# Attention units of half the tokens with both heads, and a residue-ordered copy of the second group's q and k, in a fused encoder block

## What is computed

```python
def dilated_band_attention(q, k, v, dilation, half, slopes):
...
    scores = jnp.einsum('bdhnqe,bdhnke->bdhnqk', qb, kb)
    scores = scores - slopes[None, None, :, None, None, None] * dist
    scores = jnp.where(valid, scores, NEG_INF)
    m = jnp.max(scores, axis=-1, keepdims=True)
    p = jnp.exp(scores - m)
    den = jnp.sum(p, axis=-1, keepdims=True)
    out = jnp.einsum('bdhnqk,bdhnke->bdhnqe', p, vb) / den
    lse = (m + jnp.log(den))[..., 0]
```

## Time and profile before

| | |
|---|---|
| median of 3 runs | 3403.81 us (3403.66 to 3404.89) |
| profiled execution | 3403.46 us, its span 3401.7 us |
| TensorE matmul busy | 3296.8 us, 97% |
| TensorE weight load busy | 2727.4 us, 80% |
| VectorE busy | 1846.6 us, 54% |
| ScalarE busy | 1301.9 us, 38% |
| GpSimd busy | 1578.1 us, 46% |
| DMA, share of 16 engines | 40.8% |

### The profile page before, as it was taken

How to read it: one execution, slowest core, us unless ns; L and a number is a source line. 1 busy time by engine, 2 the same in 40 slices (tenths; PEclk the granted TensorE clock), 3 DMA queues, 4 the chain that set the end, 5 groups by cost and what they waited for, 6 DMA issues and landing times.

```text
span 3401.7 us, 42068 instructions
## 1 busy us (share of the span) xinstructions
PE 3296.8 (97%) x15943; PEld 2727.4 (80%) x15943; DVE 1846.6 (54%) x2336; ACT 1301.9 (38%) x2131; POOL 1578.1 (46%) x1492
## 2 busy tenths in 40 slices
PE   7999999999889999999899999999999999999998
PEld 6788878788578888888578878888888888888886
DVE  3665655555666777664432023456456456455556
ACT  4534344444155665663342232233233233223222
POOL 4554533333258888886365433333333323323323
PEclk9999999999899999999899999999999999999999
DMA  5444453433355555554543323332332333323323
GB/s 170 129 142 141 142 154 116 120 112 90 91 143 136 148 135 140 125 128 122 201 143 113 123 75 100 118 106 87 112 99 88 117 93 104 107 87 111 111 81 106
DMA packets 666051, 405.06 MB, mean 119 GB/s; under 512 B 193534, under 2 KB 597178, under 8 KB 665338
## 3 DMA queue, kind: packets, MB, share of 16 engines
q1 hardware_dynamic: 665850, 402.38, 40.8%
HBM read 347.05 MB, written 54.53 MB: 118 GB/s over the span
## 4 chain that ended last, share of the span: by engine, by line
PE 49%; DVE 1%; ACT 0%; issue 0%; POOL 0%; DVEq 0%; ACTq 0%; POOLq 0%
PE f_bank L2194 9%; PE f_bank L2195 9%; PE f_bank L2196 9%; PE f_bank L2232 4%; PE f_bank L2233 4%; PE f_bank L2234 4%; PE f_bank L2172 2%; PE f_bank L2174 2%; PE f_bank L2173 2%; PE f_bank L2115 1%; PE f_bank L2116 1%; PE f_bank L2117 1%; PE f_bank L2124 0%; PE f_bank L2150 0%; DVE orw_plain L2688 0%
## 5 line engine op out<-in xcount | busy, mean ns | idle before, releaser
L2483 POOL TENSOR_TENSOR w_lo_b<-w_raw_b,w_hi_b 128x1024 fp32r<-128x1024 f32 x176 | 435.7, 2479 | 903.9 <-ACT w_hi_b L2359 903.7
L2194 PE MATMUL f_bank<-act_rounded,w_lo_b 128*128 128x512 f32 x1408 | 549.3, 390 | 1.2 <-DVE act_rounded L2595 1.2
L2195 PE MATMUL f_bank<-act_rounded,w_hi_b 128*128 128x512 f32 x1408 | 548.0, 389 | 0.0
L2196 PE MATMUL f_bank<-act_rounded,w_hi_b 128*128 128x512 f32 x1408 | 547.9, 389 | 0.0
L1294 POOL TENSOR_TENSOR ring_w_rounded<-ring_w_plain,ring_w_hi 128x1024 fp32r<-128x1024 f32 x134 | 327.3, 2447 | 463.1 <-ACT ring_w_hi L1310 463.0
L1622 PE MATMUL slab_ps<-h_hi,ring_w_rounded 128*128 128x512 f32 x1056 | 426.2, 404 | 2.7 <-DVE h_lo L1451 2.4
L1623 PE MATMUL slab_ps<-h_lo,ring_w_hi 128*128 128x512 f32 x1056 | 414.6, 393 | 0.0
L1624 PE MATMUL slab_ps<-h_hi,ring_w_hi 128*128 128x512 f32 x1056 | 414.1, 392 | 0.0
L2359 ACT CAST w_hi_b<-w_raw_b 128x1024 fp32r<-128x1024 f32 x176 | 185.0, 1052 | 452.9 <-DMA w_raw_b<-in_w_ffn_up_dram 207.1
L2194 PEld LDWEIGHTS f_bank<-act_rounded,w_lo_b 128*128 128x128 f32 x1408 | 264.7, 188 | 56.0 <-DVE act_rounded L2595 1.1
L2196 PEld LDWEIGHTS f_bank<-act_rounded,w_hi_b 128*128 128x128 f32 x1408 | 264.5, 188 | 55.1
(11 more groups left out here) (432 smaller groups left out, 6234.7 us busy)
## 6 DMA issues: line engine op xcount, KB each, us to landing
ring_w_plain<-in_w_in_dram SPq DMA_DIRECT2D x190, 512.0 KB, 4.1
w_raw_b<-in_w_ffn_gate_dram SPq DMA_DIRECT2D x88, 512.0 KB, 3.7
w_raw_b<-in_w_ffn_up_dram SPq DMA_DIRECT2D x88, 512.0 KB, 3.7
w_raw_b<-in_w_ffn_down_dram SPq DMA_DIRECT2D x42, 512.0 KB, 4.1
w_raw_b<-in_w_out_dram SPq DMA_DIRECT2D x16, 1024.0 KB, 5.1
zt<-slab_out SPq DMA_DIRECT2D x63, 256.0 KB, 4.3
hid_plain<-in_w_ffn_down_dram SPq DMA_DIRECT2D x21, 512.0 KB, 4.5
oa_plain<-in_w_ffn_down_dram SPq DMA_DIRECT2D x21, 512.0 KB, 4.3
```

Source lines behind the costliest of these rows:

```text
L2194: pe.matmul(o, wl[:, k, :], act_hi[:, kk, :], start=kk == 0, stop=False)
L2195: pe.matmul(o, wh[:, k, :], act_lo[:, kk, :], start=False, stop=False)
L2196: return pe.matmul(o, wh[:, k, :], act_hi[:, kk, :], start=False, stop=stop)
L2483: pool.tensor_tensor(low(r), slab_raw(j % 2), high(r).bitcast(F32), ALU.subtract).then_inc(slab_low, 1)
```

## The change

1. A unit is now half of the tokens (`half`, blocks `2 * half` and `2 * half + 1`) of both heads of a pair. The number of units and of matmuls per unit stays. In `scores` and `sum` the head `e` runs in the innermost loop, so neighbouring matmuls use rows (or output columns) 0 to 63 and 64 to 127 in turn. The scores of head `e`, block `i` go to `sc_ps[:, 2 * e + i]`.
2. `soft` does one addition per head (and for the first group per block), `exp` stays at four exponentials, and `file` copies 128 partitions x 256 tokens.
3. A new ScalarE stage `by_four`, once per pair behind `by_residue`, copies the second group's q and k by residue modulo 4 to `q_4` and `k_4`. It waits for `qk_landed[1]` and, from pair 1 on, for the last scores of the second group of the pair before. The scores of the second group read the copies and wait for `by_four` in place of the loads.
4. `sel_r` lies in the same place as `sel`; its copy at the start remains.

```diff
     if n is not None and n % ATT_PER_PAIR == 0:
-        stages.append(("by_residue", n // ATT_PER_PAIR))
+        stages += [("by_residue", n // ATT_PER_PAIR), ("by_four", n // ATT_PER_PAIR)]
...
+        q_4, k_4 = sb("q_4", [P, SEQ]), sb("k_4", [P, SEQ])
...
+                        if name == "by_four":
+                            act.wait_ge(qk_landed[1], 32 * (n + 1))
+                            if n:
+                                act.wait_ge(made, PE_DONE["scores", ATT_PER_PAIR * n - 3])
+                            for src, dst in ((q_sb, q_4), (k_sb, k_4)):
+                                ins = act.copy(dst[:, :].rearrange("p (r m) -> p r m", r=4),
+                                               src[1][:, :].rearrange("p (m r) -> p r m", r=4))
+                            ins.then_inc(taken_act, 1)
...
-                            for t in range(4):
-                                ins = act.activation(p_sb[n % 2][:, t, 0:nk], s_sb[:, t, 0:nk], ACT.Exp, bias=negmax[n % 2][:, t:t + 1],
-                                                     accum_out=dn_all[gr][:, 2 * j + e, t:t + 1])
+                            for e in range(2):
+                                for i in range(2):
+                                    x, t = 2 * e + i, 2 * half + i
+                                    ins = act.activation(p_sb[n % 2][:, x, 0:nk], s_sb[:, x, 0:nk], ACT.Exp, bias=negmax[n % 2][:, x:x + 1],
+                                                         accum_out=dn_all[gr][:, 2 * j + e, t:t + 1])
...
-                            parts = ([(0, 1, 0), (1, 3, 1), (3, 4, 2)] if gr == 0 else [(0, 4, 2 + gr)])
+                            for e in range(2):
+                                parts = [(0, 1, half), (1, 2, 1 + half)] if gr == 0 else [(0, 2, 2 + gr)]
...
-                            o = u_all[gr][r, j, :]
+                            o, src = u_all[gr][:, j, :], pv_ps[:, half * 2 * P:(half + 1) * 2 * P]
                             if gr == 0:
-                                dve.tensor_copy(o, pv_ps[r, :]).then_inc(taken_dve, 1)
+                                dve.tensor_copy(o[:, half * 2 * P:(half + 1) * 2 * P], src).then_inc(taken_dve, 1)
                             else:
-                                res = 4 if gr == 1 else 16
+                                res = 2 if gr == 1 else 8
...
-                            for t in range(4):
-                                if gr == 0:
-                                    w = windows(t)
-                                    ins = pe.matmul(sc_ps[:, t, :], q_sb[0][r, t * P:(t + 1) * P], k_sb[0][r, w:w + 2 * P], start=True, stop=True)
-                                else:
-                                    ins = pe.matmul(sc_ps[:, t, 0:P], tokens((q_sb[1], q_r)[gr - 1][r, :], gr, t),
-                                                    tokens((k_sb[1], k_r)[gr - 1][r, :], gr, t), start=True, stop=True)
+                            q_t, k_t = ((q_sb[0], k_sb[0]), (q_4, k_4), (q_r, k_r))[gr]
+                            for i in range(2):
+                                t = 2 * half + i
+                                at, nk = (windows(t), 2 * P) if gr == 0 else (t * P, P)
+                                for e in range(2):
+                                    r = slice(64 * e, 64 * e + 64)
+                                    ins = pe.matmul(sc_ps[:, 2 * e + i, 0:nk], q_t[r, t * P:(t + 1) * P], k_t[r, at:at + nk], start=True, stop=True)
...
-                            for t in range(4):
+                            for i in range(2):
+                                t = 2 * half + i
                                 for b in range(nb):
                                     vi = vstarts(0).index(windows(t) + b * P) if gr == 0 else t
-                                    ins = pe.matmul(pv_ps[64 * e:64 * e + 64, t * P:(t + 1) * P], v_tok[gr][:, vi, 64 * e:64 * e + 64],
-                                                    p_t[:, t * nb + b, :], start=b == 0, stop=b == nb - 1, skip_group_check=True)
+                                    for e in range(2):
+                                        ins = pe.matmul(pv_ps[64 * e:64 * e + 64, t * P:(t + 1) * P], v_tok[gr][:, vi, 64 * e:64 * e + 64],
+                                                        p_t[:, (2 * e + i) * nb + b, :], start=b == 0, stop=b == nb - 1, skip_group_check=True)
...
-            g.sel = c0.enter_context(nc.sbuf_tensor("sel", [ATTN_HPG, ATTN_HPG, HEAD_DIM], F32))
+            g.sel_r, g.sel = two_faced(nc, c0, "sel", [ATTN_HPG, ATTN_HPG, HEAD_DIM])
```

More of the change, by code:

```diff
@@ L1055, in phase_project @@
         floor, y, t_sb, kk_out = (sb(n, [P, SEQ]) for n in ("n_floor", "n_y", "n_t", "kk_out"))
-        sq_hi, ones_r, sel_r = sb("n_sq_hi", [P, SEQ], F32R), sb("ones_r", [P, P], F32R), sb("sel_r", [ATTN_HPG, ATTN_HPG * HEAD_DIM], F32R)
+        sq_hi, ones_r = sb("n_sq_hi", [P, SEQ], F32R), sb("ones_r", [P, P], F32R)
         with ExitStack() as early:
@@ L1337, in _ @@
                 act.wait_ge(att_consts, 2)
-                act.copy(sel_r[:, :], g.sel[:, :, :].rearrange("h a b -> h (a b)")).then_inc(sums_ready, 1)
+                act.copy(g.sel_r[:, :, :], g.sel[:, :, :]).then_inc(sums_ready, 1)
                 for s in range(N_SLOT):
                     for name, n in pro_act(s):
-                        if name == "by_residue":
+                        if name == "by_four":
[6 more added lines that the diff above has]
+                            ins.then_inc(taken_act, 1)
+                        elif name == "by_residue":
                             act.wait_ge(qk_landed[2], 48 * (n + 1))
@@ L1544, in _ @@
                         elif name == "soft":
-                            j, gr, e = att_unit(n)
-                            nk, h = 2 * P if gr == 0 else P, 2 * j + e
+                            j, gr, half = att_unit(n)
+                            nk = 2 * P if gr == 0 else P
                             dve.wait_ge(made, PE_DONE["scores", n])
@@ L1549, in _ @@
                                 dve.wait_ge(taken_act, ACT_DONE["exp", n - 1])
-                            parts = ([(0, 1, 0), (1, 3, 1), (3, 4, 2)] if gr == 0 else [(0, 4, 2 + gr)])
[L1551 to L1555, removed]
+                            for e in range(2):
+                                parts = [(0, 1, half), (1, 2, 1 + half)] if gr == 0 else [(0, 2, 2 + gr)]
+                                for a0, a1, dj in parts:
+                                    a0, a1 = 2 * e + a0, 2 * e + a1
+                                    ins = dve.scalar_tensor_tensor(out=s_sb[:, a0:a1, 0:nk],
+                                                                   in0=g.dist[:, dj:dj + 1, 0:nk].broadcast_to([P, a1 - a0, nk]),
+                                                                   scalar=g.slope[:, gr, 2 * j + e:2 * j + e + 1], in1=sc_ps[:, a0:a1, 0:nk],
+                                                                   op0=ALU.mult, op1=ALU.add)
@@ L1556, in _ @@
                             link(ins)
-                            link(dve.tensor_reduce(mx_all[gr][:, h, :], s_sb[:, :, 0:nk], AX.X, ALU.max))
-                            dve.tensor_scalar(negmax[n % 2][:, :], mx_all[gr][:, h, :], -1.0, None, ALU.mult).then_inc(taken_dve, 1)
+                            top = mx_all[gr][:, 2 * j:2 * j + 2, 2 * half:2 * half + 2]
+                            link(dve.tensor_reduce(top, s_sb[:, :, 0:nk].rearrange("p (e i) k -> p e i k", e=2), AX.X, ALU.max))
+                            dve.tensor_scalar(negmax[n % 2][:, :].rearrange("p (e i) -> p e i", e=2), top, -1.0, None, ALU.mult).then_inc(taken_dve, 1)
@@ L1689, in _ @@
                         elif name == "scores":
[L1690 to L1693, removed]
+                            j, gr, half = att_unit(n)
+                            if gr == 0:
+                                pe.wait_ge(qk_landed[0], 32 * (j + 1))
                             else:
-                                pe.wait_ge(taken_act, ACT_DONE["by_residue", j])
+                                pe.wait_ge(taken_act, ACT_DONE["by_four" if gr == 1 else "by_residue", j])
                             if n >= 1:
@@ L1746, in _ @@
                             pe.wait_ge(taken_dve, DVE_DONE["weigh", n - 4] if n >= 4 else DVE_DONE["share", 0])
-                            heads = sel_r[:, 2 * j * HEAD_DIM:(2 * j + 2) * HEAD_DIM]
+                            heads = g.sel_r[:, 2 * j:2 * j + 2, :].rearrange("h a b -> h (a b)")
                             pe.matmul(four_banks[n % 4], heads, m_lo[gr], start=True, stop=False)
```

12 lines of the change are left out of this document (5 added, 7 removed).

## The result

The changed kernel takes 3366.45 us (median of 4 runs, 3361.01 to 3370.11) against 3404.22 for the kernel before (3403.66 to 3404.89): ratio 0.9889, interval 0.9877 to 0.9901. That is 38 us less, where 22 were forecast (3382) with a range of 3372 to 3397. It is the rival "full overlap", for which the text worked out 3368 and gave a chance of 0.08.

A forecast was written before the change was run, and what follows sets the result against it. The prediction took TensorE to bound the kernel from 477 to 836 us and summed 3403.5 - 8.6 (copies) - 14.1 (both heads in a unit) + 1.0 (given back) = 3381.8, rounded 3382 us, range 3372 to 3397.

The forecast's parts named there:

- full overlap: Scores and sums: both heads' matmuls run side by side as if one, each stage takes half its passes; 3368 us, chance 0.08.
- What bounds the kernel: From 477 to 836 us TensorE is busy 357.8 of 359 us, so only its work or waits reaching it count.
- the rival in which the gain doesn't reach the end: Slots with five copies: ScalarE arrives last, TensorE waits for squares or weights; 3403 us minus at most 2, chance 0.05.
- Term 1: Second group's scores: contiguous q and k copies cut a stage from 2.48 to 1.40 us, 8.6 us less on TensorE.
- Term 2: Scores and sums: both heads in one unit, alternating array halves, overlap partly at changes of half; 14.1 us less.
- partial overlap: The forecast itself: passes in scores and sums overlap only in part where the half changes; 3374 to 3388 us, chance 0.54.
- The rival without overlap: Scores and sums: passes finish one after the other whatever the half, only the copies gain; 3395.9 us, chance 0.27.
- Term 3: VectorE: additions cost 4.6 us more, filing about 10 us less; net -5 us, nothing on the path.
- Term 5: Wait ahead of the sums of squares, laid to ScalarE: TensorE's savings there turn into wait, about 1 us given back.
- The slower rival: Scores and sums: each of 176 changes of half empties TensorE at 0.23 us, 40.5 us more; 3436 us, chance 0.06.

The follow-up runs named there:

- head-by-head run: The changed kernel with the head as the outer loop in scores and sums, so the array half changes once per stage; 3368.9 us median, ratio 0.9909.

## Why the prediction was wrong

- **What bounds the kernel** (TensorE from 477 us on): right. Nearly all that the stages lost came off the path, 33.5 of 35.8 us at the last sums, so the rival in which the gain doesn't reach the end falls.
- **Term 1, the copies, 8.6 us**: right as it was worked out, 8.7 us in the kernel before. Added to a full pairing it would have been counted too high, since beside pairing the copies are worth 4.3. ScalarE's copies took 1.13 us each and hid, as said.
- **Term 2, both heads, 14.1 us**: this is the term that was mis-sized; it measured 27.3 (stages of 104.9 us with the copies alone, 77.6 with both). The mechanism was right, its reach was not. Two steps failed. "The two passes of one matmul use the same half, so neighbours in the order can pair up only at a change" took the order of the program for an order of starts across both halves; each half starts its own passes, in the head-by-head run past three waiting passes of the other. And the weight loads were taken to come one after the other, which made me give the scores with equal load and stream nothing; they load side by side. On the rule of the Trainium skill (TensorEngine Tiling (Array Packing), Key Properties: tiles load and multiply in parallel) these runs agree to 7 ns a stage. They agree with what the same section of the Trainium skill says of a change of mode too: 0.24 to 0.30 us stay at the edge of a stage, where the size of the tile changes, and do not appear where only the half does.
- **The chances**: full overlap had 0.08 and was the outcome. That its 3368 lies 1.6 us from the median of 3366.45 is partly luck: it counts 35.6 us off, of which the traces show 33.5 at the last sums, and the other 4 of the medians' 38 are unexplained. The argument against it rested on no row, only on how I thought the queue works, and with no row on either side partial overlap should not have had seven times its chance. The range, from 3372 on, then left out this rival's own time. The rival without overlap, 0.27, falls: the stages would have stayed at 104.9 us.
- **Term 3, VectorE**: filing 22.4 to 13.1 us, 9.2 less where about 10 were said; the additions cost about 5 more. Hidden.
- **Term 5, given back, 1 us**: right for the wait (0.9 us more), though the chain was read one link short: behind ScalarE's squares stands GpSimd's subtraction of 1.6 us, and TensorE waits for that. That a wait of 2.1 us would be followed by 3.4 us at half the clock, another 1.4 us, was not foreseen; in the kernel before, 1.23 us of wait at the same place had no such fall, and neither had 1.61 us in the head-by-head kernel.
- **The slower rival**: excluded. No cost of a change of half could be seen.

## What to carry to other kernels

Two matmuls of 64 rows on different row halves, or of 64 columns on different column halves, cost what one costs, if both are in the same stage and no more than four passes of one half (two plain fp32 matmuls) stand ahead of the other's; with eight ahead part of it was lost, and between the two nothing was tried. So give a unit of work both halves, and fewer blocks of each. Copying a strided operand to contiguous order pays even on a busy chip when another engine has room, but it saves less where passes already overlap. When a stage gets much shorter, look for the chain of another engine that now ends last: moving two instructions of ScalarE ahead took another 3.6 us off the stretch, in one trace. And take a second trace of each kernel before giving the change what lies outside it: here two executions of one kernel differed by 8 us.

## What the runs showed of the hardware

- A half of the array is worked off independently: the first pass of the other half begins 7 ns behind with the halves in turn, 13 ns behind four passes, 493 ns behind eight.
- Strided passes (a step of four fp32) pair as well: 10.4 us busy for 64 of them instead of 17.9, each as long as alone (412 ns, 594 for a first one).
- TensorE's clock stood at its lower level for 61 to 92 us of an execution in the eleven traces, in falls of 3.4 to 27 us. The same kernel's time moved with it: by 8.3 us between traces with 92 and 61 us, and by 16 us over eleven runs with mean clocks of 0.986 to 0.991.
- Column halves write one bank at the same time without loss: sums of both heads into `pv_ps` take 1.342 us, of one head 1.335.
